# Split squares for the head sums of na_in: two one-pass products each, means ahead of low weight parts, another bank for chunk 3

## The reference, cut to what matters

```python
def _heads(h, w, g=None):
    b, n, _ = h.shape
    t = (h @ w).reshape(b, n, -1, HEAD_DIM)      # HEAD_DIM = 64, 16 heads
    return t if g is None else _rms(t, g)

q = _heads(hx, w[:, :hd], na_q_g[j])             # 256 tokens
k = _heads(hx, w[:, hd:2 * hd], na_k_g[j])
v = _heads(hx, w[:, 2 * hd:])
k_c, v_c = _heads(hc, ...), _heads(hc, ...)      # 256 context tokens
x = x + gx1 * (_neighbourhood_attention(q, k, v, k_c, v_c, na_rpb[j]) @ na_w_out[j])
```

## Time and profile before

| | |
|---|---|
| median of three runs | 1294.21 us (1294.12 to 1294.3) |
| profiled execution | 1294.86 us, its span 1293.1 us |
| busy over the span | PE 1275.7 (99%), PEld 1097.0 (85%), DVE 964.6 (75%), ACT 594.9 (46%), POOL 424.9 (33%) |
| chain that ended last | PE 75%, DVE 14%, issue 5%, DMA 2%, ACT 2%, POOL 1% |
| DMA | 219.96 MB, mean 170 GB/s |

### The profile page before, as it was taken

One profiled execution on the slowest core, in us unless ns is written; L12 is line 12 of the kernel. 1 busy time (PEld: TensorE's weight loads), 2 busy tenths in 40 slices (PEclk: granted clock), 3 DMA queues, 4 the chain that ended last, 5 costly groups with the idle time before them and its releaser, 6 DMA issues.

```text
span 1293.1 us, 19800 instructions
## 1 busy us (share of the span) xinstructions
PE 1275.7 (99%) x7680; PEld 1097.0 (85%) x7680; DVE 964.6 (75%) x1380; ACT 594.9 (46%) x968; POOL 424.9 (33%) x416
## 2 busy tenths in 40 slices
PE   8999999999999999999999999999999999999999
PEld 8888989999888888888788787888767777998887
DVE  6688698999987898897667476566677766977553
ACT  6237556666653233444211243223555554766432
POOL 1562131333330002365200266012466552454100
PEclk9999999999999999999999999999999999999999
DMA  9774466555663553354456365563232332555552
GB/s 306 264 262 157 151 211 199 181 180 186 205 214 112 188 207 126 115 170 159 148 194 194 116 226 210 189 228 127 107 107 73 115 98 70 183 187 186 190 182 79
DMA packets 66268, 219.96 MB, mean 170 GB/s; under 512 B 9120, under 2 KB 12448, under 8 KB 66176
## 3 DMA queue, kind: packets, MB, share of 16 engines
q1 hardware_dynamic: 65888, 218.46, 50.3%
q10 hardware_dynamic: 288, 0.25, 0.1%
HBM read 217.21 MB, written 1.05 MB: 169 GB/s over the span
## 4 chain that ended last, share of the span: by engine, by line
PE 75%; DVE 14%; issue 5%; DMA 2%; ACT 2%; POOL 1%; SPq 0%; DVEq 0%; ACTq 0%; POOLq 0%
PE ps L634 15%; PE ps L648 15%; PE ps L646 15%; PE ps L624 11%; PE ps L626 6%; DVE wlo L1917 4%; DVE tmp L2207 2%; DMA raw<-in_w_in 2%; DVE Y L1944 1%; PE ps L1225 1%; PE ps L1252 1%; PE ps L1239 1%; DVE modsum L1999 1%; PE ps L1218 1%; PE ps L718 1%
## 5 line engine op out<-in xcount | busy, mean ns | idle before, releaser
L1401 ACT ACTIVATE whi<-raw 128x1024 fp32r<-128x1024 f32 (+1 forms) x302 | 317.3, 1052 | 305.5 <-DMA raw<-in_w_0b 73.7
L634 PE MATMUL ps<-A,whi 128*128 128x256 f32 (+2 forms) x1332 | 440.4, 331 | 0.8 <-ACT sq L1844 0.8
L1917 DVE TENSOR_TENSOR wlo<-raw,whi 128x1024 fp32r<-128x1024 f32 (+1 forms) x302 | 400.8, 1332 | 47.7 <-ACT whi L1401 47.7
L648 PE MATMUL ps<-A,wlo 128*128 128x256 f32 (+2 forms) x1312 | 422.9, 322 | 1.7 <-DVE wlo L1917 1.7
L646 PE MATMUL ps<-A,whi 128*128 128x256 f32 (+2 forms) x1312 | 422.4, 322 | 0.2 <-DVE A L1930 0.2
L634 PEld LDWEIGHTS ps<-A,whi 128*128 128x128 f32 x1332 | 253.0, 190 | 41.6 <-issue 18.5
L648 PEld LDWEIGHTS ps<-A,wlo 128*128 128x128 f32 x1312 | 249.2, 190 | 21.8 <-DVE wlo L1917 2.5
L646 PEld LDWEIGHTS ps<-A,whi 128*128 128x128 f32 x1312 | 249.4, 190 | 20.2 <-issue 1.7
L1999 DVE SCALAR_TENSOR_TENSOR modsum<-raw,cond,modsum 128x1024 f32<-128x1024 f32 x98 | 154.4, 1605 | 0.0
L624 PE MATMUL ps<-H,whi 128*128 128x512 f32 x400 | 141.8, 399 | 0.2 <-POOL H L2672 0.2
L2672 POOL TENSOR_TENSOR H<-tmp,H 128x256 fp32r<-128x256 f32 (+1 forms) x86 | 111.9, 1301 | 88.7 <-ACT H L1736 75.1
(11 more groups left out here) (369 smaller groups left out, 1846.5 us busy)
## 6 DMA issues: line engine op xcount, KB each, us to landing
raw<-in_ada SPq DMA_DIRECT2D x96, 512.0 KB, 4.0
raw<-in_w SPq DMA_DIRECT2D x64, 512.0 KB, 3.5
raw<-in_w_up SPq DMA_DIRECT2D x44, 512.0 KB, 3.5
raw<-in_w_in SPq DMA_DIRECT2D x34, 512.0 KB, 5.9
raw<-in_w_0a SPq DMA_DIRECT2D x32, 512.0 KB, 3.8
raw<-in_w_0b SPq DMA_DIRECT2D x32, 512.0 KB, 3.6
raw<-in_na_in SPq DMA_DIRECT2D x24, 512.0 KB, 4.9
raw<-in_w_down SPq DMA_DIRECT2D x22, 512.0 KB, 3.5
```

Of the source, the lines that this page charges most:

```text
L634: e.matmul(o, w_hi, ah, start=k == 0, stop=False)
L648: m = e.matmul(o, w_lo, ah, start=False, stop=last)
L1401: e.activation(whi[s % NHI][:, :cols], raw[i % NRAW][:, :cols], ACT.Copy).then_inc(S("whi").sem, 1)
L1917: e.tensor_tensor(wlo[i % NRAW][:, :cols], raw[i % NRAW][:, :cols], plain(whi[s % NHI][:, :cols]), SUB).then_inc(S("wlo").sem, 1)
```

## The change

The square of a k or q chunk is split as weights are: ACT copies `sq` rounded to fp32r into `sq_hi`, DVE writes the rest to `sq_lo`. The head sum becomes two one-pass products with an fp32r copy of `blocks`, which ACT makes once behind the first square. DVE's `square_low` stands in `after_na`, behind `turned2` and ahead of `scores2`. The mean stands ahead of `los` at n = 4 and after every chunk with scores (5, 6, 8, 9, 10, 11, 13, 14, 15, 16, 18, 19, 21, 22). Chunk 3 uses bank 3, which waits for the last part of the stage before; `product2` waits at its first use that chunk 3 has been read from it.

```diff
-APART = {..., ("pool_w", 3): 4, ("na_out", 3): 4, ...}
+APART = {..., ("pool_w", 3): 4, ("na_in", 3): 3, ("na_out", 3): 4, ...}
...
+    sq_hi = [sb(f"sq_hi{i}", 512, f32r, at=h_at + 51200 + 2048 * i) for i in range(2)]
+    sq_lo = [sb(f"sq_lo{i}", 512, f32r, at=h_at + 55296 + 2048 * i) for i in range(2)]
+    blocks = sb("blocks", 128, f32r, at=h_at + 59392)
...  bank_free
+            elif (name, n) == ("na_in", 3):
+                w.wait_ge(S("d0b_r"), 16)
...  TensorE
-        def head_sum(j, src, T, n):
-            w.wait_ge(S("na"), n + 1)
+        def head_sum(j, T):
+            w.wait_ge(S("blocks"), 1)
+            w.wait_ge(S("sq_hi"), j + 1)
             o = turn_bank("norm", j)[:, :T]
-            e.matmul(o, const("blocks"), src, start=True, stop=True).then_inc(S("hn_sum").sem, 1)
+            e.matmul(o, blocks, sq_hi[j % 2][:, :T], start=True, stop=False)
+            w.wait_ge(S("sq_lo"), j + 1)
+            e.matmul(o, blocks, sq_lo[j % 2][:, :T], start=False, stop=True).then_inc(S("hn_sum").sem, 1)
...  product2
             if p:
                 w.wait_ge(S("o2"), p)
+            else:
+                w.wait_ge(S("na"), 4)
...  ACT
                     e.activation(sqr[:, :T], o[:, :T], ACT.Square).then_inc(S("na").sem, 1)
+                    if n == 0:
+                        e.activation(blocks, const("blocks"), ACT.Copy).then_inc(S("blocks").sem, 1)
+                    w.wait_ge(S("na"), n + 1)
+                    e.activation(sq_hi[j % 2][:, :T], sqr[:, :T], ACT.Copy).then_inc(S("sq_hi").sem, 1)
...  DVE
+        def square_low(n):
+            if norm2(n):
+                j, _, T = norm2(n)
+                w.wait_ge(S("sq_hi"), j + 1)
+                if j >= 2:
+                    w.wait_ge(S("hn_sum"), j - 1)
+                e.tensor_tensor(sq_lo[j % 2][:, :T], sq[j % 2][:, :T], plain(sq_hi[j % 2][:, :T]), SUB).then_inc(S("sq_lo").sem, 1)
...  DVE, after_na(u)
+            square_low(u)
             if scores:
                 scores2(*scores)
...  DVE, order of the stage
+        MEAN_FIRST = [4, *(u + 1 for u in scores_after if 4 < u + 1 < 24)]
-            if n > 4:
+            if n > 4 and n not in MEAN_FIRST:
                 mean_of(n - 1)
...
-                if i == 4:
-                    mean_of(3)
+                if i in MEAN_FIRST:
+                    mean_of(i - 1)
                 if i:
                     los(UNIT["na_in", i])
```

More of the change, by code:

```diff
@@ L99 @@
              "w1_0b": "r0b", "w2_0b": "d0b_r", "na_in": "na", "na_out": "nao_r", "w1_1": "r1", "w2_1": "d1_r"}
-APART = {("w_in", 3): 3, ("w_in", 4): 5, ("w_in", 5): 7, ("pool_w", 1): 5, ("pool_w", 3): 4, ("na_out", 3): 4, ("na_out", 4): 5, ("na_out", 5): 7}
+APART = {("w_in", 3): 3, ("w_in", 4): 5, ("w_in", 5): 7, ("pool_w", 1): 5, ("pool_w", 3): 4, ("na_in", 3): 3, ("na_out", 3): 4, ("na_out", 4): 5, ("na_out", 5): 7}
 NRAW, NHI = 9, 4
@@ L1260, in during_na @@
                     j, _, T = norm2(m)
-                    head_sum(j, sq[j % 2][:, :T], T, m)
+                    head_sum(j, T)
                 else:
```

## The result

The changed kernel takes 1299.53 us (median of 7 runs, 1297.19 to 1302.57), the kernel before beside it 1294.30 (1294.12 to 1295.78): ratio 1.0043, 95% interval 1.0033 to 1.0052. The forecast was 1295.5, no change; the time lies above the whole range given. The spread of the times, 5.4 us against 1.7 before, is a weaker sign: in those groups of 17 to 24 runs the kernel before spreads by 3.0 to 4.6 us, and one run of the changed kernel took 1300.29 with a clock of 0.999.

The account below looks back on a forecast made before the run. TensorE's own instructions bound late na_in, while early it waits; queue waits less savings summed to +1.25 us: 1295.5 from the median 1294.21, called no change. Own range 1293.5 to 1297.5, whole range 1291.5 to 1299.0.

Parts of the forecast that it names:

- Step 1: Chunk 3: its third product waits for wlo(3), now behind square_low(0); lag +1.97, or +1.58 after the head sum's saving.
- Step 4: Scores pairs (0,0) and (0,1) run in 1.13 each, giving back 1.1 and 1.75 us; lag falls to +2.65.
- step 2: Chunk 4: sq_lo(1) stands ahead of wlo(4), which runs 924.7 to 925.9; lag +2.8.
- step 3: Sum of chunk 3: its second product waits for sq_lo behind head_out(1); lag +5.7, TensorE idle some 4 us.
- step 5: Sum of chunk 5 waits for the bank DVE empties in scores2(0,1), now behind sq_lo; lag +3.7 behind it.
- Step 6: Rest of the stage: later sums and pair (2,1) give back 2.45 net of waits; end lag +1.25.
- the clock: Rival, chance 0.12: TensorE's clock falls to 1.2 GHz after the idle time in chunk 3's sum, adding 2.8 us: 1298.3.
- the walk: The prediction's six steps through na_in's queues, following TensorE's lag from chunk 3 to the end: +1.25 us.
- DVE keeps the lag: Rival, chance 0.20: DVE's added sq_lo work lets the late sums give nothing back; lag stays +3.7, 1297.9.
- "faster" rival: Rival, chance 0.15: only TensorE's work counts in na_in, ACT and DVE hide the split; 5.5 us saved, 1288.7.

Follow-up runs that it names:

- fill_newton0: Changed kernel with 11, 2 and 6 useless products in TensorE's three gaps and GpSimd's Newton steps for chunk 0's sum cut to 32 of 512 columns: 1295.83 us.
- fill_bank: Changed kernel with 11, 8 and 7 useless products in TensorE's three gaps and the sums of chunks 4, 5 and 10 back in float32: 1298.46 us.
- after: The changed kernel itself, against the kernel before: 1299.53 us median; its profile is of the fastest of seven runs, 1297.19 us.
- fill3: Changed kernel with 11, 8 and 7 useless products in TensorE's waits ahead of chunks 3 and 4 and in the sum of chunk 3: 1298.15 us.
- again: The changed kernel timed once more, nothing altered: 1300.01 us, ratio 1.0033 to 1.0058 against the kernel before.
- first_two: Changed kernel with the sums of chunks 0 and 1 back as one float32 product, the other fourteen split: 1297.20 us.
- newton0_cut: Changed kernel with GpSimd's Newton steps for the sum of chunk 0 on only 32 of 512 columns, gaps not filled: 1296.73 us.
- split_alone: Changed kernel with the means in their old places and chunk 3 in its old bank, only the split sums left: 1303.32 us.
- chunk3_f32: Changed kernel with the sum of chunk 3 alone back as one float32 product, the others split: 1300.13 us.
- late13_order: Changed kernel with the sums of chunks 0, 1 and 3 in float32 and sq_lo moved behind the score bank reads in scores2: 1299.76 us.
- late10: Changed kernel with the sums of chunks 0, 1, 3, 4, 5 and 10 in float32, ten split: 1290.98 us.
- late11_b: Changed kernel with the sums of chunks 0, 1, 3, 5 and 10 in float32, eleven split: 1292.54 us.

## Why the prediction was wrong

**Right: the order.** Each wait came where steps 1 to 6 put it, with two short ones beside them in the sum of chunk 1 (0.38 and 0.26). Step 1: lag +1.97 predicted, 916.81 - 916.40 + 1.59 = 2.00 measured. Step 4's pairs take 1.13. The sums save what was said where nothing waits: 0.36 to 0.41 for 512 columns (lag 4.69 after that of chunk 8, 5.07 before it), 0.2 for 256.

**Wrong, the sizes in steps 2, 3 and 6.** The end lag was to be +1.25 and is +4.19:
- Steps 2 and 3, 1.1 of the 2.9. "wlo(4), which runs 924.7 to 925.9" took 2.29, and chunk 4 has 925.78 - 923.14 + 1.59 = 4.2 instead of +2.8. Before, wlo(4) ran at 920.35, ahead of the Newton steps, and the row of 2.14 in the earlier trace rows is wlo(5), beside them; step 2 moved wlo(4) into their time and took its price from the quiet row. TensorE then stood 1.97 us in the sum of chunk 3 and not some 4. What step 3 waits for, head_out(1), hangs on GpSimd, which pays for the meeting too: its last product for the sum of chunk 0 started 0.3 behind wlo(5) and took 2.13, where it had 1.27 before. Its next steps so have a lag of 928.37 + 1.59 - 927.38 = 2.58 (the first ones 1.69), head_out(1) has 2.57 instead of 1.58, and behind the sum the lag is 933.53 - 928.31 + 1.59 = 6.8 instead of +5.7. VectorE and GpSimd before:

```profile
920.35 1.21 DVE L1917 TENSOR_TENSOR wlo<-raw,whi 128x1024 fp32r<-128x1024 f32 x1
...
921.85 2.66 POOL L2822 TENSOR_TENSOR tmp<-tmp,tmp 128x512 f32<-128x512 f32 x2 [12.49 <-ACT tmp L1796]
...
926.15 1.27 POOL L2826 TENSOR_TENSOR tmp<-tmp,tmp 128x512 f32<-128x512 f32 x1
...
927.38 1.87 POOL L2822 TENSOR_TENSOR tmp<-tmp,tmp 128x256 f32<-128x256 f32 x2
```

  The Trainium skill's rule on shared SBUF interfaces (GPSIMD Engine Reference, section 8, Key points), with which these numbers agree, was weighed for sq_lo alone and not for the two instructions that set the lag. Where the meeting was taken away, with the first Newton steps (fill_newton0), the time is 1295.83.
- Steps 4 and 5, 0.4: TensorE came to the sum of chunk 5 at +4.1 rather than +2.65, and it left with 5.65 - 0.39 = 5.3 rather than +3.7. (In step 4, 937.60 to 940.43 less 1.13 is 1.70 and not 1.75.)
- Step 6, 1.4: it gives back 1.1, not 2.45. The sum of chunk 10 waits 1.33 where 0.53 was taken; the wait for ada is 0.72 against 0.19 before, which costs 0.14 more than the 0.39 that step 6 gave up for it; and another 0.37 goes ahead of the sum of chunk 19, where product2(4) now has a short wait of its own (0.3, listed as issue: for nothing that the profile shows). Of the 1.33, sq_lo of chunk 10 itself is 0.6 by fill_bank. The rest is VectorE's queue ahead of it, and one mis-sized term there is sq_lo: the split was to add 5.4 us to the 80.82, and the twelve sq_lo between 940.40 and 1056 took 10.3, those of 256 columns 0.98 each where 0.3 was taken (groups by line and shape of after in that window):

```profile
L2531 DVE TENSOR_TENSOR sq_lo<-sq,sq_hi 128x256 fp32r<-128x256 f32 x6 | 5.9, 980 | 0.6 <-ACT sq_hi L1858 0.5
L2531 DVE TENSOR_TENSOR sq_lo<-sq,sq_hi 128x512 fp32r<-128x512 f32 x6 | 4.4, 728 | 0.2 <-ACT sq_hi L1858 0.2
```

**Wrong, the chance of the clock.** The rival had 0.12, with a fall behind step 3 alone. In the changed kernel the fall differs from run to run and costs 1.4 to 1.9 in the median (fill3 against after and again); the slowest run is 5 above fill3's median, though not all of that need be the clock. first_two shows it whole, at 2.7. Idle times of 2.9, 1.6 and 2.0 us stand close together in after, and no row of before could show what they do to the clock. Which gap the fall follows in the runs of 1302 us no profile shows; in the profiles of after and again it is chunk 4's, in newton0_cut's chunk 3's, in those of split_alone and chunk3_f32 there is a fall behind either. In after's profile it cost nothing, as said at fill3, so the end lag is without it.

**The sum, in medians:** 1294.4 before; +1.3 by the walk as predicted; +2.4 for what steps 2 to 6 were short of (that is fill3's 3.7 less the 1.3; the lags of the two profiles give 2.9); +1.4 to 1.9 by the clock: 1299.5 to 1300. The rival "DVE keeps the lag" had 1297.9 and comes near fill3's 1298.15, but its reason is half right: step 6 did give back 1.1. The "faster" rival (0.15) falls with the result, and late13_order shows that the other place for sq_lo doesn't save it: its nine waits for sq_lo come to 9.7 us.

## What to carry to other kernels

A saving on the bounding engine is worth what the queues of its feeders leave of it: sum up, between two waits, what each feeder has in line, and price an instruction that moves by what it will run beside, not by where its row stood. Split only where the feeder has slack; here one sum of 256 columns cost seven to eight times its saving (late10 against late11_b). And weigh a new idle gap on TensorE twice: for itself, and for the products behind it, which may run at half the clock. Here that was 2.7 us behind the gap of first_two, and nothing in the profile of after, where what followed had to wait anyway.

## Of the hardware, not expected

- The clock's fall isn't the same from run to run: behind the same wait of 2.9 us in chunk 3 the granted clock stayed 1.00 in the profiles of after and again and was 0.77 in newton0_cut's (915 to 920 us). Means over 11 runs of first_two, with its one long gap, were nearly all 0.997.
- Useless products in a wait make the kernel faster: 1297.20 to 1294.49 in first_two.
- Where VectorE and GpSimd met, the one that started second paid in these rows of after: wlo(4) at 923.44, with GpSimd at work since 921.95, took 2.29; GpSimd's product at 926.29, behind wlo(5) at 925.98, took 2.13, and that wlo 1.29.
- A short VectorE instruction may cost more than a long one: the eight sq_lo of 256 columns all ran beside GpSimd and took 0.89 on average (0.61 to 1.24), those of 512 columns, six of which met GpSimd for less than 0.1 us, 0.72 (groups by line and shape of after, busy us and mean ns):

```profile
L2531 DVE TENSOR_TENSOR sq_lo<-sq,sq_hi 128x256 fp32r<-128x256 f32 x8 | 7.1, 888 | 3.5 <-ACT sq_hi L1858 3.4
L2531 DVE TENSOR_TENSOR sq_lo<-sq,sq_hi 128x512 fp32r<-128x512 f32 x8 | 5.8, 719 | 4.3 <-ACT sq_hi L1858 4.3
```
